# RWKV recurrence in a new order with 32x32 inverse blocks and quarter pairs, HGRN side products at other row tiles

## The reference, cut to what matters

```
sa = S @ (-kk_t)
S  = S * w_t + sa (x) b_t + v_t (x) k_t
y  = S @ r_t            # then group norm, bonus, gate by silu(z)
```

## Time and profile before

| | |
|---|---|
| runs | 3361.74, 3362.47, 3368.26 us |
| profiled execution | 3362.26 us, span 3360.5 us |
| TensorE (PE) busy | 2986.1 us, 89% of the span |
| weight loads (PEld) busy | 2782.1 us, 83% |
| VectorE (DVE) busy | 1318.7 us, 39% |
| ScalarE (ACT) busy | 1124.8 us, 33% |
| GpSimd (POOL) busy | 130.6 us, 4% |
| mean granted TensorE clock | 0.957 |
| RWKV dense | from 0 to 871.7 us |
| RWKV recurrence | from 871.7 to 1706.0 us |
| first output projection | from 1706.0 to 2046.0 us |
| HGRN | from 2046.0 to 3078.0 us |
| second output projection | from 3078.0 to 3360.5 us |

### The profile page before, as it was taken

One profiled execution on the slowest core, in us unless ns is written; L12 is line 12 of the kernel. 1 busy time (PEld: TensorE's weight loads), 2 busy tenths in 40 slices (PEclk: granted clock), 3 DMA queues, 4 the chain that ended last, 5 costly groups with the idle time before them and its releaser, 6 DMA issues. The chain is left out here.

```text
span 3360.5 us, 81805 instructions
## 1 busy us (share of the span) xinstructions
PE 2986.1 (89%) x37120; PEld 2782.1 (83%) x37120; DVE 1318.7 (39%) x2139; ACT 1124.8 (33%) x1557; POOL 130.6 (4%) x123
## 2 busy tenths in 40 slices
PE   5999999999688888888859948999999999996993
PEld 4999999999677777777759928999999999996993
DVE  4343333221355665566521154343333334333113
ACT  5343333322144343343322233333333333333221
POOL 0000000000000000000000010000000000000001
PEclk8999999999799999999979968999999999997997
DMA  2333333332111111111132153222232222223222
GB/s 107 105 105 112 112 112 112 112 112 100 43 48 44 42 45 43 45 42 44 37 133 88 47 191 128 77 95 80 87 103 80 87 88 88 91 78 118 76 84 97
DMA packets 91238, 288.85 MB, mean 86 GB/s; under 512 B 18721, under 2 KB 25249, under 8 KB 70433
## 3 DMA queue, kind: packets, MB, share of 16 engines
q1 hardware_dynamic: 79136, 257.19, 22.3%
q10 hardware_dynamic: 9216, 17.83, 1.4%
q0 software_dynamic: 2560, 8.91, 0.7%
HBM read 229.56 MB, written 54.34 MB: 84 GB/s over the span
## 5 line engine op out<-in xcount | busy, mean ns | idle before, releaser
L134 PE MATMUL ab_pair<-ab_x_hi,ab_w_hi 128*128 128x272 f32 x2048 | 432.9, 293 | 23.9 <-ACT ab_x_hi L303 19.2
L1225 PE MATMUL e_pair<-e_x_hi,e_w_hi 128*128 128x272 f32 x1984 | 442.2, 304 | 6.4 <-DVE e_w_lo L1500 6.4
L134 PE MATMUL ab_pair<-ab_x_hi,ab_w_lo 128*128 128x272 f32 x2048 | 425.5, 289 | 0.0
L134 PE MATMUL ab_pair<-ab_x_lo,ab_w_hi 128*128 128x272 f32 x2048 | 424.3, 289 | 0.0
L1225 PE MATMUL e_pair<-e_x_hi,e_w_lo 128*128 128x272 f32 x1984 | 415.2, 291 | 0.0
L1225 PE MATMUL e_pair<-e_x_lo,e_w_hi 128*128 128x272 f32 x1984 | 414.3, 291 | 0.0
L346 DVE TENSOR_TENSOR ab_w_lo<-ab_raw,ab_w_hi 128x2048 fp32r<-128x2048 f32 x64 | 146.6, 2293 | 524.2 <-ACT ab_w_hi L278 524.2
L134 PEld LDWEIGHTS ab_pair<-ab_x_hi,ab_w_hi 128*128 128x128 f32 x2048 | 325.9, 189 | 29.6 <-issue 21.0
L1225 PEld LDWEIGHTS e_pair<-e_x_hi,e_w_hi 128*128 128x128 f32 x1984 | 313.4, 191 | 39.3 <-issue 32.0
L134 PEld LDWEIGHTS ab_pair<-ab_x_lo,ab_w_hi 128*128 128x128 f32 x2048 | 323.6, 190 | 0.0
L134 PEld LDWEIGHTS ab_pair<-ab_x_hi,ab_w_lo 128*128 128x128 f32 x2048 | 321.7, 190 | 0.0
(11 more groups left out here) (327 smaller groups left out, 4799.1 us busy)
## 6 DMA issues: line engine op xcount, KB each, us to landing
ab_raw<-in_w_in SPq DMA_DIRECT2D x64, 1024.0 KB, 4.8
e_raw<-in_hgrn_in SPq DMA_DIRECT2D x64, 1024.0 KB, 4.8
o_raw<-in_rwkv_wo SPq DMA_DIRECT2D x16, 1024.0 KB, 4.8
o_raw<-in_hgrn_wo SPq DMA_DIRECT2D x16, 1024.0 KB, 4.7
o_o<-scr_yz SPq DMA_DIRECT2D x32, 272.0 KB, 9.0
e_Ss<-in_hgrn_s SPq DMA_DIRECT2D x16, 512.0 KB, 4.7
out_hgrn_s<-e_Sd SPq DMA_DIRECT2D x16, 512.0 KB, 7.0
ab_nxt<-in_x SPq DMA_DIRECT2D x4, 1088.0 KB, 9.2
```

The source lines that it names most:

```text
L134: mm = pe.matmul(out[:, a, 0:TH], w, x[:, kt, a * TH:(a + 1) * TH], start=(kt == 0 and n == 0), stop=(kt == KT - 1 and n == 2))
L1225: mm = pe.matmul(out[:, a, 0:TH], w, x[:, kt, a * TH:(a + 1) * TH], start=(kt == 0 and i == 0), stop=(kt == KT - 1 and i == 2))
```

## The change

Recurrence of RWKV:

- The loop becomes `for i in range(-2, KT)` with three pairs in flight: back i, front j = i + 1, ahead h = i + 2 (key norm and the first low-rank product of the pair after next). The level steps of the front stand between the links of the state chain of the back. The samples' steps move from front to back, except for their first products. `kt`, `kkn` get two buffers; loads and stores move to other places in SyncE's queue.
- The doubling works inside 32x32 blocks: `pTiT`, `pTi`, `pX` hold 256 columns, a level is four 32x32 products for each chunk, on the diagonal of the array, for each of the two halves. Four levels are done this way. GpSimd spreads the blocks into `TiT` (`diagonal`). The corner of each 64x64 inverse is then `corner_x`, a copy, `corner_yt`, and two ScalarE copies.
- Products are issued in "quarter pairs": with two groups of products, one in the two diagonal quarters of the array and the other in the two swapped quarters, into two banks, `channel_pair` and `token_pair`. `strict` mixes 32-column products (blocks of MT) with 64x64 quarters.

HGRN: `sample_out` is cut in four parts (two sequences each), keyed 3, 4, 5, 6; `sample_state` moves from 5 and 8 to 8 and 10, `norm` from 12 to 13; in tile 4e + 3 `v_by_token` moves from 5 to 3, `level` 6 from 4 to 6, `level` 7 from 7 to 9, `k_by_token` from 10 to 12, `kv` from 13 to 15.

```diff
-        NL = len(RWKV_LEVELS)
+        NL = len(RWKV_LEVELS) - 1
+        HC = C // 2
-        MT, Mak, Mrb, Mrk, TiT, Ti, X = (sb(n, [P, SEQ]) for n in (...))
+        MT, Mak, Mrb, Mrk, TiT = (sb(n, [P, SEQ]) for n in ("MT", "Mak", "Mrb", "Mrk", "TiT"))
+        pTiT, pTi, pX = (sb(n, [P, SEQ // 2]) for n in ("pTiT", "pTi", "pX"))
-        b0, b1, y_ps, m_ps = (ps(n, [P, 512]) for n in ("b0", "b1", "y", "m"))
+        l_ps, c0_ps, c1_ps, f_ps, y_ps, m_ps = (ps(n, [P, 512]) for n in ("l", "c0", "c1", "f", "y", "m"))
...
+            def quarter(out, o_half, lhsT, rhs, i_half, start=True, stop=True):
+                return pe.matmul(out[rows(o_half)], lhsT[rows(i_half)], rhs[rows(i_half)], start=start, stop=stop,
+                                 skip_group_check=not (start and stop))
+            def channel_pair(same, l_same, r_same, swapped, l_swap, r_swap):
                 for c in range(NCH):
-                    mm = stacked(cut(out, c), cut(src, c), k.eye)
+                    for hh in range(2):
+                        quarter(cut(same, c), hh, cut(l_same, c), r_same if r_same is k.eye else cut(r_same, c), hh)
+                        mm = quarter(cut(swapped, c), 1 - hh, cut(l_swap, c),
+                                     r_swap if r_swap is k.eye else cut(r_swap, c), hh)
+            def strict(j):
+                for c in range(NCH):
+                    for hh in range(2):
+                        for half in range(2):
+                            at0 = c * C + HC * half
+                            pe.matmul(cut(c1_ps, c)[q32(2 * hh + half)], b[rows(hh), at0:at0 + HC],
+                                      a[rows(hh), at0:at0 + C], start=True, stop=True)
+                        mm = quarter(cut(f_ps, c), 1 - hh, cut(kt, c), cut(a, c), hh)
             def level_x(j, l):
-                chunks(b1, MT, Ti).then_inc(s.x_mm, 1)
+                for c in range(NCH):
+                    for g in range(4):
+                        mm = pe.matmul(half_cut(l_ps, c)[q32(g)], MT[q32(g), c * C:c * C + HC],
+                                       half_cut(pTi, c)[q32(g)], start=True, stop=True)
...
+            for i in range(-2, KT):
+                j, h = i + 1, i + 2
+                back, front, ahead = i >= 0, 0 <= j < KT, h < KT
+                if front:
+                    rank_a(j)
+                if back:
+                    sample_step(i, 0)
+                    first_right(i)
+                    sample_step(i, 1)
+                    sample_step(i, 2)
+                    g_and_value_y(i)
+                    u_and_value_state(i)
+                if front:
+                    bonus(j)
+                if back:
+                    rho_rest(i)
+                    u_state(i)
+                    sample_states(i)
+                    chain(i, 1)
+                if front:
+                    strict(j)
+                if back:
+                    chain(i, 2)
+                if ahead:
+                    square_sum(h)
+                if back:
+                    chain(i, 3)
+                    sample_y(i)
+                if front:
                     level_x(j, 1)
+                if back:
+                    u_y(range(4, NCH))
+                    state_y(i, 3)
+                    chain(i, 4)
+                    state_y(i, 2)
+                    state_y(i, 1)
+                if front:
                     level_yt(j, 1)
+                    b_and_k_by_token(j)
+                if back:
+                    chain(i, 5)
+                if front:
                     level_x(j, 2)
...
+                if front:
+                    a_and_v_by_token(j)
                     level_x(j, 3)
+                if back:
+                    mean(i)
+                if front:
                     level_yt(j, 3)
+                    samples(j)
+                if back:
+                    variance(i)
+                if front:
                     level_x(j, 4)
+                    inclusive(j)
                     level_yt(j, 4)
+                if ahead:
+                    rank_w(h)
+                if back:
+                    chain(i, 7)
+                if front:
+                    corner_x(j)
+                    sample_right(j)
+                    corner_yt(j)
...
             def late(e):
-                return {1: lambda: outputs(e, 0), 2: lambda: outputs(e, 2), 3: lambda: sample_out(e),
-                        5: lambda: sample_state(e, 0), 8: lambda: sample_state(e, 1), 12: lambda: norm(e)}
+                return {1: lambda: outputs(e, 0), 2: lambda: outputs(e, 2), 3: lambda: sample_out(e, 0),
+                        4: lambda: sample_out(e, 1), 5: lambda: sample_out(e, 2), 6: lambda: sample_out(e, 3),
+                        8: lambda: sample_state(e, 0), 10: lambda: sample_state(e, 1), 13: lambda: norm(e)}
...
-                dense(4 * e + 3, {1: L(5), 4: L(6), 5: lambda: v_by_token(e), 7: L(7), 10: lambda: k_by_token(e),
-                                  13: lambda: kv(e)})
+                dense(4 * e + 3, {1: L(5), 3: lambda: v_by_token(e), 6: L(6), 9: L(7), 12: lambda: k_by_token(e),
+                                  15: lambda: kv(e)})
```

More of the change, by code:

```diff
@@ new lines, in chain, with u_y, state_y @@
+            def chain(i, c):
+                pe.wait_ge(s.state, NCH * i + c)
+                stacked(cut(c0_ps, c), cut(G, c), cut(S, c - 1)).then_inc(s.chain_mm, 1)
+            def u_y(c_range):
+                for c in c_range:
+                    mm = stacked(cut(y_ps, c), cut(U0, c), cut(Mrb, c), False, c == 0)
+                return mm
+            def state_y(i, c):
+                pe.wait_ge(s.rhoe, i + 1)
+                pe.wait_ge(s.state, NCH * i + c)
+                return stacked(cut(y_ps, c), cut(S, c - 1), cut(rhoE, c), False, True)
@@ L867, in _, with corner @@
+                if back:
[4 more added lines that the diff above has]
+                    corner_yt(j)
         @block.scalar
         def _(act):
+            def corner(i):
+                act.wait_ge(s.yt_mm, NL * (i + 1))
+                act.wait_ge(s.diag, i + 1)
+                for hh in range(2):
+                    act.copy(by_chunk(TiT)[q32(2 * hh)][:, :, HC:], by_half(l_ps)[q32(2 * hh)]).then_inc(s.corner, 1)
@@ L888, in _ @@
+                    corner(i)
                 if front:
@@ new lines, in _ @@
+                if back:
+                    link(i, 3)
+                if ahead:
+                    dve.wait_ge(s.ss_mm, h + 1)
+                    dve.tensor_scalar(halves(rn[:, :]), q[:, :, 0:TH], 1e-24, None, ALU.max).then_inc(s.ssm, 1)
+                if front:
+                    mask_x(j, 1)
+                    dve.tensor_tensor(by_chunk(Mak), by_chunk(f_ps), each(k.strict), ALU.mult).then_inc(s.mak, 1)
+                if back:
+                    link(i, 4)
+                if front:
+                    add_tit(j, 1)
+                    turn_ti(j, 1)
@@ new lines, in _ @@
+                if back:
+                    link(i, 5)
+                if front:
+                    mask_x(j, 2)
+                if back:
+                    link(i, 6)
+                if front:
+                    add_tit(j, 2)
+                    turn_ti(j, 2)
+                if ahead:
+                    dve.wait_ge(s.rn, h + 1)
+                    dve.scalar_tensor_tensor(kkn[h % 2][:, :], kt_[h % 2][:, :], par(params, "k_k", h), rn[:, :],
+                                             ALU.mult, ALU.mult).then_inc(s.kkn, 1)
@@ L1661, in constants @@
     t["eye"] = twice(np.eye(C))
-    t["lev1"] = twice(level_t(one, 1, 1))
-    for m in RWKV_LEVELS[1:]:
-        t[f"lev{m}"] = twice(level_t(one, 1, m).T)
     tt = one - SMP
@@ L1683, in constants @@
         t[f"h_lev{m}"] = four(level_t(i32, 1, m))
+    for m in RWKV_LEVELS[1:5]:
+        t[f"p_lev{m}"] = four(level_t(i32, 1, m).T)
+    part = (i32[:, None] < i32[None, :]) * 1.0
+    t["bdiag"] = np.kron(np.tile(np.eye(2), (2, 1)), np.ones((32, 32)))
+    t["strict32"] = np.tile(np.concatenate([np.concatenate([part, np.ones((32, 32))], 1),
+                                            np.concatenate([part, np.zeros((32, 32))], 1)]), (2, 1))
     t["h_seq"] = pad((u[:, None] // DS == np.arange(NB)[None, :]) * 1.0)
```

672 lines of the change are left out of this document (360 added, 312 removed).

## The result

The changed kernel takes 3399.2 us (median of 4 runs, 3391.9 to 3405.1); the kernel before, run beside it, 3362.1 us (3358.8 to 3368.3). The ratio is 1.011, with a 95% interval of 1.008 to 1.013: slower by 1.1%. The forecast was 3110 us, range 3035 to 3215. The profiled execution took 3405.1 us, its span is 3403.3.

A forecast was written before the change was run, and what follows sets the result against it. The tensor engine was taken to bound the recurrence, by work and by waiting. Steps of 35 us in place of 49.75 give 221 us less, HGRN 31 less: 3362.3 to 3110 us, range 3035 to 3215.

The forecast's parts named there:

- The new order: Recurrence: level chain and state chain hide each other; 1.5 us of tensor engine standing left in a step.
- 33.6: Recurrence: summed tensor work of one new step in us, where it was 39.1.
- 10.7 us beyond issue time: Recurrence before the change: part of a 49.75 us step in which the tensor engine stands, beside 39.1 us of issue.
- `strict` 2.4 us: Recurrence step: 96 records of `strict` with 32 tile-size changes, middle between 0.9 and 4.1 us.
- `strict` over 4 us: Sign in the profile, listed beforehand, that would show the forecast wrong.
- half the tiles are the same rows of the array: `strict`: argument for taking the middle, 2.4 us, for its tile-size changes instead of the high end, 4.1.
- the forecast of 35: Recurrence: loop step of 33.6 us tensor work plus 1.5 us standing, 35 us used, in place of 49.75.
- the clock falls: Rival, recurrence: small level tiles count as idle and work goes at half rate; up to 3616 us; chance 0.05.
- levels in single file: Rival: a level's four row tiles write one bank, so records go singly; step 48 us, 3305 us; chance 0.06.
- Quarters do not overlap beyond two: Rival: quarter pairs run only two at once and `strict` pays each change; step 42 us, 3215 us; chance 0.15.
- the split: HGRN's 31 us less: 24 from covering the level 6 wait, 7 of a possible 15 from splitting the samples' product.
- the first front: Recurrence's start, 55.9 us before: some 5 us less, set against some 5 us more at the last back.

The follow-up runs named there:

- 64x64 blocks: Changed kernel with its new order and alternating quarter pairs kept, but the inverse on 64x64 blocks as in the kernel before: 3134.3 us, ratio 0.932.
- quarters two at a time: Changed kernel put back on 64x64 blocks, with each quarter pair's two sets of products issued one after the other instead of alternating: 3163.6 us, ratio 0.941.
- `strict` in two groups: Changed kernel with all 32-column products of `strict` issued first, then all 64x64 quarters, same instructions: 3245.5 us, ratio 0.965.
- 16 groups: Changed kernel with `strict` ordered by chunk, four 32-column products then two quarters, 16 tile-size changes in place of 32: 3287.0 us, ratio 0.977.
- with the waits: Changed kernel with `strict` regrouped by tile size, plus two waits for a long-reached count ahead of each level product: 3636.1 us, ratio 1.081.
- the row moves alone: Kernel before with only HGRN's level 6, level 7, products by token and `kv` moved to other row tiles: 3357.6 us, ratio 0.9975.

## Why the prediction was wrong

From the kernel before to the changed one by way of the experiments, each row the difference of two medians:

| edit | us |
|---|---|
| HGRN edits | -36 |
| new order of the recurrence, 64x64 blocks, quarters two at a time | -163 |
| quarter pairs alternating | -29 |
| 32x32 blocks (`strict` in two groups) | +111 |
| `strict` alternating between tile sizes | +154 |
| sum of the unrounded rows | +36 |

The changed kernel measured +37 beside the kernel before. That the rows add up to it proves nothing about them, since each begins where another ends; only the HGRN row was measured apart. Another order of the edits would share the time out otherwise.

- **The new order** did what was forecast: the level chain and the state chain hide each other. The waits of the tensor engine went from 6.8 us a step (94.5/14, 973 to 1673) to 2.2 (30.9/14, 64x64 blocks). With that run's own terms (33.6 less 11.0 for `strict`, half levels and corner, plus 1.0 and ten times 0.98) the sum is 33.4 + 2.2 = 35.6 us; 37.05 were measured, so that the prediction's 10.7 us beyond issue time are 3.7 by the same sum.
- **The step that failed first** is the term "`strict` 2.4 us", with its high end of 4.1. It takes 9.8, of which 7.8 would be left at full clock. I took 0.1 us a change, though my own rows from HGRN had 0.09 us ahead of a level and 0.2 behind it, 0.15 a change. Here each of the 32 groups takes 0.245 us to the next; against 2.17 us in two groups that is 0.19 us for each of the 30 changes more, and 0.14 with 16 groups. "`strict` over 4 us" stood among the signs of a wrong forecast, and it was the right place to look; the argument "half the tiles are the same rows of the array" had no row behind it. The rule that the Trainium skill gives (TensorEngine Tiling (Array Packing), "Key Properties": changing the tiling mode drains the TensorE) held, in that no two groups of different size overlapped by more than 0.08 us; the time, 7.8 us at full clock, is nearly twice my upper bound of 4.1.
- **The step that was missing** is the supply of instructions. My counts add up to 1344 records a step and took a smaller number of nanoseconds as a saving. Below 29 to 33 ns a record, on average over some hundreds, a shorter record saves nothing: 1344 x 29 = 39 us, an estimate of the floor from the 3.75 us a block above, is over the forecast of 35, and 43.6 were measured with `strict` repaired. No rival held it. No row of the kernel before shows such a floor, but one division would have raised the question: 49.75/1056 = 47 ns was the rate before, and 35/1344 = 26 ns the rate that I forecast, which no whole step had come near.
- **The rival "the clock falls"** came true in part; whether by the cause that it named is open. The steps have 0.80. That the small tiles lower it by themselves is not shown, and not refuted: a level group at full clock stands above, but every kernel with 32x32 products is under 1 (0.91, 0.76, 0.65, and 0.62 with the waits), and those with 64x64 blocks are at 1.00. Gaps alone don't explain it: the kernel before stood 6.8 us a step at 1.00, and the one with the waits has no gaps at 0.62. In the changed kernel it fell inside `strict`, with 70 records in 8 us, and, with `strict` in two groups, next to the gaps. From 35: + 7.4 (`strict`) + 5.1 (gaps) - 0.8 (other waits, 0.7 against 1.5) leaves 7.4 us of 54.1 for the clock, worked out as the remainder. That is near 0.20 x 54.1 = 10.8 us of lost clock, less some 2 us inside `strict` (9.8 less 7.8) and 1 in the gaps. How the clock is granted is not settled by these runs.
- **The rival "levels in single file"** is refuted: 64 records in 0.68 us. The Trainium skill (TensorEngine Tiling (Array Packing), "Gotcha 1: PSUM Pressure") states that different row tiles cannot access the same bank at the same time; for four row tiles too the trace disagrees. **"Quarters do not overlap beyond two"** is refuted by 14.7 ns a record, and by the 29 us that the alternation is worth.
- **HGRN** was right in sum, 35 for 31. The wait was 22 us for 24. But the split was wrong as a statement of what each edit gives: the row moves alone gave 7 us (12 in the profiled run), since the lost clock grew to 27 us, and the other edits, the spread of the samples' product among them, gave the rest. Their term was 7 of a possible 15; they are worth all 15 and the 12 more that the row moves would have cost.
- **Edges**: the first front was costed at 5 us less. Up to the first store of `yz`, which takes in a whole step as well, the recurrence takes 20 us more (121.2 against 101.3), and a step explains some 4 of them. The clock is 0.56 in the first 56 us, where `strict` alone takes some 12 us; it was 0.72 before.

## What to carry to other kernels

Before a product is cut into smaller ones, divide the time that is forecast by the number of instructions: over some hundreds of instructions in a row the tensor engine has a floor per instruction, apart from its work. Its mark are "issue" gaps at even distances, each of which ends shortly after a packet of the instruction queue has landed. Products on different tile sizes belong in as few groups as can be: the price is per change, not per product. An edit's gain in waits can be eaten by the clock, so read the granted clock of the stretch beside the wait that went away.

## What the runs showed of the hardware

- One block of 256 instructions (16 KB) came each 3.75 us in a stretch of level groups, and each 4.13 to 4.27 us on average in three kernels that were short of them: 29 ns, and 32.5 to 33.5 ns, for a matmul and its weight load. Up to 2.5 us of gap stood in one place, and the gaps over 0.8 us ended 1.2 to 1.6 us after a block had landed.
- With changes between 32-column and 64-column tiles on both sides, a group takes 0.23 to 0.26 us to the next one at 2.4 GHz, 0.35 to 0.40 at 1.2 GHz, for two to eight records alike.
- A wait of its own between small products, for a count long reached, took 86 ns in a level group at 1.2 GHz.
- The granted clock was 0.62 in a kernel whose tensor engine counts as busy for 953.5 of 961 us (the one with waits), and 1.00 in one with 486.7 of 519 (64x64 blocks).
